# Expert-key layer of a two-block transformer: picked indices and a counting row in PSUM, one first low half, gate products one tile behind

## The reference, cut to what matters

```
v1, i1 = top_k(s1, 16);  v2, i2 = top_k(s2, 16)
cand = v1[..., :, None] + v2[..., None, :]
top_s, pos = top_k(cand, 16)
experts = i1[pos // 16] * 128 + i2[pos % 16]
gates = softmax(top_s)
act = gelu(u_tab[experts] . x) * gates
out = sum(act * v_tab[experts])
```

## Time and profile before

| what | value |
|---|---|
| median of 3 runs | 2225.16 us (2223.81 to 2225.94) |
| the profiled execution's own time | 2225.21 us |
| span of the profiled execution | 2223.5 us |
| PE busy | 2095.4 us, 94% |
| DVE busy | 1608.0 us, 72% |
| ACT busy | 1130.4 us, 51% |
| POOL busy | 694.6 us, 31% |
| query stage's last matmul ends | 1415.56 us |
| early tiles | 1421.49 to 1615.87 us |
| gate stage, from unit 0 | 1626.52 to 1862.93 us |
| value part's matmuls | 1862.93 to about 2216 us |

### The profile page before, as it was taken

One profiled execution on the slowest core, in us unless ns is written; L12 is line 12 of the kernel. 1 busy time (PEld: TensorE's weight loads), 2 busy tenths in 40 slices (PEclk: granted clock), 3 DMA queues, 4 the chain that ended last, 5 costly groups with the idle time before them and its releaser, 6 DMA issues. The chain is left out here.

```text
span 2223.5 us, 33708 instructions
## 1 busy us (share of the span) xinstructions
PE 2095.4 (94%) x11228; PEld 1722.0 (77%) x11228; DVE 1608.0 (72%) x2587; ACT 1130.4 (51%) x1641; POOL 694.6 (31%) x468
## 2 busy tenths in 40 slices
PE   5989999997999999999999999889899999999998
PEld 4875767775877776777776657889899999888887
DVE  4367888887367878888879741499589997555555
ACT  5353767774335367777550323345444444444544
POOL 6620040001757504000030005599967773000000
PEclk9999999999999989999999999999999999999999
DMA  9864889995457648999832333245444445555554
GB/s 396 303 230 152 306 307 357 343 347 196 180 199 288 261 177 324 339 344 343 335 101 95 123 113 133 95 162 187 160 133 141 141 141 182 191 193 189 189 190 150
DMA packets 76634, 485.70 MB, mean 218 GB/s; under 512 B 9472, under 2 KB 9984, under 8 KB 58624
## 3 DMA queue, kind: packets, MB, share of 16 engines
q1 hardware_dynamic: 75824, 482.88, 60.4%
q10 hardware_dynamic: 720, 1.61, 0.2%
HBM read 483.41 MB, written 1.05 MB: 218 GB/s over the span
## 5 line engine op out<-in xcount | busy, mean ns | idle before, releaser
L1198 DVE TENSOR_TENSOR moe_w_lo<-ring,moe_w_hi 128x1024 fp32r<-128x1024 f32 x384 | 466.8, 1252 | 50.4 <-ACT moe_w_hi L1122 36.0
L1122 ACT ACTIVATE moe_w_hi<-ring 128x1024 fp32r<-128x1024 f32 x376 | 385.1, 1058 | 73.3 <-PE bank L1055 42.1
L3097 POOL TENSOR_TENSOR peer_u_lo<-peer_u,peer_u_hi 128x512 fp32r<-128x512 f32 x253 | 343.4, 1369 | 97.1 <-ACT peer_u_hi L3122 95.5
L3037 PE MATMUL bank<-peer_hn_hi,peer_u_hi 128*128 128x256 f32 x1024 | 296.0, 289 | 17.9 <-POOL peer_u_lo L3097 12.0
L3038 PE MATMUL bank<-peer_hn_lo,peer_u_hi 128*128 128x256 f32 x1024 | 287.6, 281 | 0.0
L3039 PE MATMUL bank<-peer_hn_hi,peer_u_lo 128*128 128x256 f32 x1024 | 287.2, 280 | 0.0
L229 POOL TENSOR_TENSOR ret_all_w_lo<-ring,ret_all_w_hi 128x1024 fp32r<-128x1024 f32 x64 | 158.7, 2488 | 292.4 <-ACT ret_all_w_hi L219 291.9
L3122 ACT ACTIVATE peer_u_hi<-peer_u 128x512 fp32r<-128x512 f32 x253 | 159.2, 629 | 130.5 <-PE bank L3039 121.1
L1036 PE MATMUL bank<-moe_w_hi,moe_slots_hi 128*128 128x512 f32 x512 | 210.4, 411 | 11.7 <-DVE moe_w_lo L1198 7.7
L3037 PEld LDWEIGHTS bank<-peer_hn_hi,peer_u_hi 128*128 128x128 f32 x1024 | 194.7, 190 | 20.2 <-POOL peer_u_lo L3097 13.8
L1038 PE MATMUL bank<-moe_w_hi,moe_slots_lo 128*128 128x512 f32 x512 | 201.2, 393 | 0.0
(11 more groups left out here) (519 smaller groups left out, 4591.2 us busy)
## 6 DMA issues: line engine op xcount, KB each, us to landing
ring<-in_stream SPq DMA_DIRECT2D x135, 2048.0 KB, 8.3
peer_u<-in_peer_u SPq DMA_DIRECT2D x128, 512.0 KB, 3.2
peer_scores<-in_peer_v SPq DMA_DIRECT2D x86, 512.0 KB, 4.3
sb_mod_ring<-in_ada_t SPq DMA_DIRECT2D x64, 512.0 KB, 6.3
peer_u<-in_peer_v SPq DMA_DIRECT2D x42, 512.0 KB, 4.3
ret_mod_ring<-in_ada_t SPq DMA_DIRECT2D x32, 512.0 KB, 5.1
s_bz<-in_b_channel SPq DMA_DIRECT2D x4, 512.0 KB, 6.9
ring<-in_stream SPq DMA_DIRECT2D x2, 1024.0 KB, 5.2
```

The lines of the kernel that those rows point to most:

```text
L1122: act.activation(w_hi[:, q, :], K.ring[:, at % RING, q * CHUNK // Q:(q + 1) * CHUNK // Q], ACT.Copy).then_inc(hi_done, 1)
L1198: dve.tensor_tensor(w_lo[:, q, :], K.ring[:, at % RING, q * CHUNK // Q:(q + 1) * CHUNK // Q], w_hi[:, q, :].bitcast(F32), ALU.subtract).th ...
L3037: pe.matmul(out, u_hi[:, b, k2, :], h_hi[:, k, :], start=(k == 0), stop=False)
L3097: pool.tensor_tensor(u_lo[:, b, :, :], u[:, i, KD // 2 * half:KD // 2 * (half + 1), :], u_hi[:, b, :, :].bitcast(F32), ALU.subtract).then_ ...
```

## The change

Five edits. (1) `idx_f` and `part_f` move from SBUF to the upper halves of PSUM banks 6 and 7. (2) ScalarE copies the counting row once to bank 5, beside the transposed row (`wide_iota`), and `a_hot` reads it from there; VectorE waits for it (`iota_there`). (3) `hot` moves from `H` to the scores' rows of the same token tile. (4) Only the first low half is made in the query stage's block (`FIRST_LOWS`), the other two at the start of GpSimd's work in the next. (5) On TensorE tile 63 goes ahead of the transposes, and each unit follows one tile later: tile 64, unit 0, tile 65, unit 1, ... tile 126, unit 62, unit 63, tile 127.

```diff
+    FIRST_LOWS = 1
     def first_low(self, pool):
-        for m in range(self.HALVES):
+        for m in range(self.FIRST_LOWS):
...
-    idx_f, cand, val, idx, best, pos, part, part_f, col, selT = first.picking
+    cand, val, idx, best, pos, part, col, selT = first.picking
+    wide_iota = K.bank[:, 5, T:T + P]
+    idx_f, part_f = (K.bank[:, 6 + i, T:2 * T].rearrange("p (a h k) -> p a h k", a=2, k=TOP) for i in range(2))
...
-    hot = H[:, PK - 8:PK, :].rearrange("p n t -> p (n t)").rearrange("p (a k j) -> p a k j", a=PK_HEADS, j=TOP)
...
             early_tiles(pe, lambda n, i, land: tile(n, i, gelu_done, n + 1))
+            tile(EARLY, 0, gelu_done, EARLY + 1)
             for r in range(3):
                 pe.wait_ge(exp_done, TT + 1)
...
-                    n = g * (2 * U_SLOTS) + (EARLY + r)
-                    tile(n, r % U_SLOTS, taken, g * (2 * U_SLOTS) + (r + 1))
+                    n = g * (2 * U_SLOTS) + (EARLY + 1 + r)
+                    tile(n, (r + 1) % U_SLOTS, taken, g * (2 * U_SLOTS) + (r + 2))
                     unit(g * (2 * U_SLOTS) + r, r % 2)
-            for r in range(EARLY // (2 * U_SLOTS) * 2 * U_SLOTS, PK - EARLY):
-                tile(EARLY + r, r % U_SLOTS, taken, r + 1)
-                if r < UNITS:
-                    unit(r, r % 2)
+            for r in range(EARLY // (2 * U_SLOTS) * 2 * U_SLOTS, UNITS):
+                if EARLY + 1 + r < PK - 1:
+                    tile(EARLY + 1 + r, (r + 1) % U_SLOTS, taken, r + 2)
+                unit(r, r % 2)
+            tile(PK - 1, (PK - 1 - EARLY) % U_SLOTS, taken, PK - EARLY)
...
-                low(n, n, 16, range(max(HALVES - 2 * n, 0), 2))
+                low(n, n, 16, range(max(first.FIRST_LOWS - 2 * n, 0), 2))
...
             act.sem_inc(gelu_done, U_SLOTS)
+            act.activation(wide_iota, K.iota, ACT.Copy).then_inc(iota_there, 1)
...
+                hot = scores[:, tt, :].rearrange("p (a k j) -> p a k j", a=PK_HEADS, j=TOP)
...
             dve.wait_ge(ones_made, 1)
+            dve.wait_ge(iota_there, 1)
...
-                    last = dve.tensor_scalar(a_hot[:, b, q, :], K.iota, selT[:, 0, one], selT[:, 1, one],
+                    last = dve.tensor_scalar(a_hot[:, b, q, :], wide_iota, selT[:, 0, one], selT[:, 1, one],
```

More of the change, by code:

```diff
@@ L2836, in __init__ @@
         self.picking = (
-            sb("idx_f", [P, 2, PK_HEADS, TOP]),
             sb("cand", [P, 2 * P]),
@@ L2843, in __init__ @@
             sb("part", [P, 2, PK_HEADS, TOP], U32),
-            sb("part_f", [P, 2, PK_HEADS, TOP]),
             sb("col", [P, 2, PK_HEADS]),
@@ L2971, in peer_stage @@
     a_hot, b_hot = (scores[:, i, 0:2 * QT * P].rearrange("p (b q i) -> p b q i", b=2, q=QT) for i in range(2))
-    hot = H[:, PK - 8:PK, :].rearrange("p n t -> p (n t)").rearrange("p (a k j) -> p a k j", a=PK_HEADS, j=TOP)
-    halves_used = s_("halves_used")
+    halves_used, iota_there = s_("halves_used"), s_("iota_there")
     turned, selT_done, a_ready, b_ready, g_made, g_used, taken, ones_made = (
```

## The result

The changed kernel takes 2203.74 us (median of four, 2201.22 to 2204.55) against 2225.15 (2223.81 to 2225.94): 21.4 us between the medians. The forecast was 18.3 us faster. The profiled execution took 2203.05 us with a span of 2201.3, 22.2 us less than before.

What follows compares the result with a forecast made beforehand. TensorE, busy 94% of the span, was taken to bound the kernel, so only its stops and half-clock stretches pay. 11.9 + 1.2 + 5.3 − 0.1 = 18.3 us off 2225.21 gave 2206.9 us, range 2203.5 to 2212.5.

Steps and rivals of the forecast that it cites:

- The eight stops of TensorE go: Early tiles: with the large operations no longer holding GpSimd, TensorE's waits for low halves vanish, 11.9 us gained.
- The 2.47 us: Seam between query stage and first tile: with one first low half TensorE restarts 2.47 us sooner.
- The new restart at 1419.02 is 0.9 us after the fall: nearest to the second: Behind the query-stage seam: clock down 6.03 us, as at the turn; 1.3 us given back, net gain 1.2 us.
- the second and third low half: Start of early tiles: both just hidden behind TensorE's matmuls; uncovered, each would cost up to 1.25 us.
- worth 5.3 us: Turn to the gate stage: tile 63 first leaves 1.5 us idle, clock stays up, unit 0 starts 2.5 us sooner.
- I priced it at 0: Gate stage: `a_hot` from PSUM takes 0.40 us, VectorE stays below 3.69 us a pair, worth 0 in the loop.
- an instruction with at most one SBUF input doesn't contend with GpSimd: Large compare and multiply: one SBUF and one PSUM input ends the turn-taking with GpSimd; the 11.9 us rests on it.
- The clock down at the turn: Rival at the transposes before the gate stage: clock down all the same, gain 15.8 us, 2209.4 us; chance 0.14.
- the half-freed case: Rival in the early tiles: only one of two large operations stops holding GpSimd, 2212.9 us; chance 0.08.
- the slower one: Rival in the gate stage: VectorE becomes the bound through `a_hot`, 2238 us at 0.60 us each; chance 0.04.
- more than forecast: Rival: clock up early after the first seam and VectorE not waited for, 2205.0 us; chance 0.09.

Runs made afterwards that it cites:

- the two part-way kernels: The kernel before with only `part_f`, then only `idx_f`, moved to PSUM: 2218.25 us and 2217.29 us.

## Why the prediction came out as it did

The direction was right and so were the mechanisms of edits 1, 3, 4 and 5; two terms of the sum had the wrong size. The median, 2203.74, lies just inside the lower end of the stated range (2203.5), the profiled execution, 2203.05, just outside.

- **Edit 1, mechanism right, size too small (the first step that failed).** "The eight stops of TensorE go", at 5.9 + 6.0 = 11.9 us, summed the idle rows. The missing matmuls, 57 and 58 in the two windows, are 13.5 us, and edit 1 alone measured 13.8. That is 1.6 to 1.9 of the surplus. Each stop costs 0.26 us more than its row, at its start and at its end, and there are eight.
- **Edit 4, the seam right, the clock wrong (the second).** The 2.47 us came as 2.45. "The new restart at 1419.02 is 0.9 us after the fall: nearest to the second" took the case with 6.03 us at 1.2 GHz and charged 1.3 us. In the profiled execution the clock did not fall, which instead gave back the 15 slow matmuls of before, 1.6 us: together 2.9 us. About 0.5 us of it went to the new stop before the fifth half (0.26 us by its row and 0.26 at its two ends). Behind the shorter seams, all four traces with the clock up have this stop, 0.22 to 0.26 us by the row, and none with the clock down. The prediction asked after the second and third low half, which were hidden as it said, and not after the fifth. So the early tiles gained 1.9 + 2.9 − 0.5 = 4.3 us more than forecast, 14.9 in place of 10.6. That the clock was up was luck: the forecast case does occur, in two of five traces of this seam. The step that failed is pricing, from two single instances, something that came out differently from trace to trace under the same code.
- **Edit 5, right, in part by luck.** Gap 1.57 us for 1.5, clock up, transposes to unit 0 in 3.66 us for 3.8, worth 5.3 us against this profile of before. That profile had the dearest of six turns; against their mean of 9.76 us it is worth 4.4.
- **Edit 2, right in the sum, wrong as a separate price.** The pair stayed at 3.69 us. I priced it at 0 and took the new `a_hot` for granted in edit 5; alone, edit 5 loses 2.5 us of its 5.3. The prediction's sentence that an instruction with at most one SBUF input doesn't contend with GpSimd fits the operations on two tensors here, but not `a_hot` of before: it has one SBUF input and took 0.331 to 1.461 us, from PSUM 0.398 to 0.408.
- **Rivals.** The clock down at the turn did not occur; the half-freed case is what each of the two part-way kernels gave; the slower one fell at 0.403 us an `a_hot`. The case nearest to the result was "more than forecast", 2205.0, and it still lacked the stops' full size: with 13.8 in place of 11.9 its sum gives 2203.1.

## What to carry to other kernels

To price a repeated stop, count the instructions missing from a window against an undisturbed one; idle rows leave out what each stop costs at its two ends, here 14% of it. An engine that keeps up on average can still be late at the ends of a stretch: before an order puts two of its consumers side by side, look at what slows it there, as edit 2 was worth 0 alone and 2.6 us under edit 5. And take a clock term behind a short stop as a spread over executions, not as a number from one profile.

## What the runs showed of the hardware that I had not expected

The granted clock can fall with TensorE already at work again: 1.00 throughout 1.83 us of idle time, then 3.4 us at 1.2 GHz in the next 8 us. The same code with the same gap of 3.5 us gave anything from 0 to 5.8 us at 1.2 GHz in five traces of four kernels, and one kernel with its gap of 2.6 us gave 0 and 3.2 us in two. And a VectorE operation that itself was not delayed, 2.29 us with both inputs in SBUF, still stopped TensorE for 1.90 us through GpSimd: GpSimd's row, not its own, shows it.
